# Entry of the short convolution: TensorE sums the meta rows, VectorE begins with tile 0

## The reference, cut to what matters

```python
h = jnp.concatenate([meta, x], axis=1)          # 16 + 512 rows
for i in range(DEPTH):
    mixed = rglru_mixer(...) if i % N_MIXERS == 0 else shortconv_mixer(...)
    h = layer_norm(ALPHA * h + mixed, ln_g[i, 0], ln_b[i, 0])
    ffn = hierarchical_moe(h, ...)              # top 2 of 32 experts per row
    h = layer_norm(ALPHA * h + ffn, ln_g[i, 1], ln_b[i, 1])
return h[:, N_META:]

def shortconv_mixer(h, w_in, conv_w, w_out):
    u = h @ w_in                                # bg | cg | v, 1024 columns each
    zc = causal_depthwise_conv(cg * v, conv_w)  # 3 taps
    return (bg * zc) @ w_out
```

## Time and profile before

| | us |
|---|---|
| median of 3 runs | 2333.53 (2333.42 to 2335.18) |
| the profiled execution | 2330.78 |
| its span, first to last instruction | 2329.1 |
| TensorE busy | 2127.1 (91%) |
| VectorE busy | 708.6 (30%) |
| ScalarE busy | 523.0 (22%) |
| GpSimd busy | 300.2 (13%) |
| mean granted clock of TensorE | 0.958 of 2.4 GHz |

### The profile page before, as it was taken

How to read it: one execution, slowest core, us unless ns; L and a number is a source line. 1 busy time by engine, 2 the same in 40 slices (tenths; PEclk the granted TensorE clock), 3 DMA queues, 4 the chain that set the end, 5 groups by cost and what they waited for, 6 DMA issues and landing times. The chain is left out here.

```text
span 2329.1 us, 28490 instructions
## 1 busy us (share of the span) xinstructions
PE 2127.1 (91%) x11572; PEld 1220.6 (52%) x11572; DVE 708.6 (30%) x1558; ACT 523.0 (22%) x1219; POOL 300.2 (13%) x306
## 2 busy tenths in 40 slices
PE   7999999999999999969999898959996999989991
PEld 3446643434545687445555454457754555545550
DVE  1055325343665455452111010151125211101104
ACT  2123221122553145112212112130001212121111
POOL 0000000221332311101111111031000111111101
PEclk9999998999999999979999999979997999999996
DMA  9315242222002222159999999962134999999993
GB/s 345 131 56 185 93 171 91 87 94 72 1 24 90 91 76 76 25 214 395 426 423 423 425 423 416 402 256 90 37 117 176 364 424 424 422 423 424 422 404 137
DMA packets 100664, 545.97 MB, mean 234 GB/s; under 512 B 13376, under 2 KB 27497, under 8 KB 66586
## 3 DMA queue, kind: packets, MB, share of 16 engines
q1 hardware_dynamic: 80950, 504.17, 53.7%
q0 software_dynamic: 19232, 39.56, 4.8%
q10 hardware_dynamic: 340, 0.28, 0.0%
HBM read 538.86 MB, written 28.94 MB: 244 GB/s over the span
## 5 line engine op out<-in xcount | busy, mean ns | idle before, releaser
L751 PE MATMUL ps<-arena,ring 128*128 128x512 f32 (+10 forms) x1968 | 589.9, 460 | 10.6 <-DVE arena L2181 2.2
L751 PEld LDWEIGHTS ps<-arena,ring 128*128 128x128 f32 (+2 forms) x1968 | 354.7, 191 | 233.9 <-issue 192.9
L1210 PE MATMUL ps<-ring,arena 128*64 128x256 f32 x3296 | 375.2, 384 | 6.1 <-ACT arena L1634 3.2
L1210 PEld LDWEIGHTS ps<-ring,arena 128*64 128x64 f32 x3296 | 233.9, 138 | 127.6 <-issue 4.6
L832 PE MATMUL ps<-ring,arena 128*128 128x512 f32 (+1 forms) x560 | 248.1, 600 | 4.9 <-ACT arena L1600 2.6
L1223 PE MATMUL ps<-ring,arena 128*64 128x512 f32 x880 | 206.0, 611 | 26.6 <-DMA ring<-in_moe_w_down_dram 26.6
L2287 DVE SCALAR_TENSOR_TENSOR arena<-arena,ps 128x256 f32<-128x256 f32 x78 | 32.8, 421 | 565.2 <-ACT arena L1644 565.2
L1210 PE MATMUL ps<-arena 128*64 128x256 f32 x1696 | 192.6, 381 | 0.0
L2564 POOL DMA_INDIRECT assignment_rows<-arena x78 | 81.6, 1046 | 797.1 <-ACT arena L1650 754.3
L832 PEld LDWEIGHTS ps<-ring,arena 128*128 128x128 f32 (+1 forms) x560 | 102.3, 186 | 137.7 <-issue 136.7
L1210 PEld LDWEIGHTS ps<-arena 128*64 128x64 f32 x1696 | 119.4, 137 | 60.5
(11 more groups left out here) (312 smaller groups left out, 1825.3 us busy)
## 6 DMA issues: line engine op xcount, KB each, us to landing
ring<-in_moe_w_down_dram SPq DMA_DIRECT2D x45, 2048.0 KB, 27.9
ring<-in_moe_w_up_dram SPq DMA_DIRECT2D x44, 2048.0 KB, 30.8
ring<-in_moe_w_gate_dram SPq DMA_DIRECT2D x43, 2048.0 KB, 25.9
arena<-in_moe_w_gate_dram SPq DMA_DIRECT2D x21, 2048.0 KB
arena<-in_moe_w_up_dram SPq DMA_DIRECT2D x20, 2048.0 KB
arena<-in_moe_w_down_dram SPq DMA_DIRECT2D x19, 2048.0 KB
ring<-in_ada_w_dram SPq DMA_DIRECT2D x12, 2048.0 KB, 8.7
ring<-in_a_w_in_dram SPq DMA_DIRECT2D x12, 1536.0 KB, 11.6
```

The costliest lines, as they stand in the source:

```text
L751: ins = pe.matmul(dst, w, m, start=i == 0, stop=i == len(pairs) - 1)
L1210: ins = pe.matmul(ps[CAP * i:CAP * (i + 1), bank_, 256 * j:256 * (j + 1)], rows_t[:, k, :], w[:, k, 256 * i:256 * (i + 1)], start=k == 0, ...
```

## The change

Tile 0 now comes first, then meta, 1, 2, 3 (`COMBINE_0`), on VectorE, ScalarE, GpSimd and for TensorE's turns; SP still loads meta's outputs first. For the meta tile VectorE's two passes are gone. Behind the routing VectorE makes two diagonal 16x16 matrices of the meta rows' gates (`meta_gates`), and TensorE, as soon as `yin[4]` has landed, sums in PSUM: identity times `X` of meta, plus each diagonal times the expert outputs, in two halves of 512 columns. VectorE takes the statistics from PSUM after tile 0's, and ScalarE normalises meta out of PSUM. ScalarE normalises every tile in two halves of 512 columns, each of which releases `normed` by 1. Its copies of tile 0 and meta stand together behind meta's normalisation, those of tile 1 behind the normalisation of tile 2, those of tiles 2 and 3 at the end. TensorE runs the early products of `cg_0` before tile 1's turn and those of `cv_0` after it; both now wait for meta's copies.

```diff
@@ -266,6 +266,7 @@
 UNITS_A = [(0, 2 * c + i, n) for c in range(GC) for n in range(NT) for i in range(2)] + \
     [(g, h, None) for g in (1, 2) for h in range(HPG)]
 NUA = len(UNITS_A)
+COMBINE_0 = (0, 4, 1, 2, 3)
 NUB = HB * NT
 
 
@@ -413,6 +414,7 @@
         slot_of = at(M0 + 20, 10).rearrange("p (t k) -> p t k", k=2)
         place = at(M0, 10 * 2)
         picked = at(M0 + 32, 2 * 5 * NE).rearrange("p (k t n) -> p k t n", k=2, n=NE)
+        meta_gates = at(R0 + 13520, 2 * META).rearrange("p (k i) -> p k i", k=2)
         emptied = at(M0 + 6400, NBLK)
         row_hot = at(M0 + 576, 10 * P).rearrange("p (i r) -> p i r", r=P)
         block_hot = at(M0 + 1856, 10 * NBLK).rearrange("p (i b) -> p i b", b=NBLK)
@@ -508,16 +510,16 @@
         def rows_of(tile):
             return META if tile == 4 else P
 
-        LN_TILES = [(l, t) for l, ts in ((0, range(4)), (1, range(4)), (2, (4, 0, 1, 2, 3)), (3, (4, 0, 1, 2, 3)),
+        LN_TILES = [(l, t) for l, ts in ((0, range(4)), (1, range(4)), (2, (4, 0, 1, 2, 3)), (3, COMBINE_0),
                                          (4, range(4)), (5, range(4))) for t in ts]
         LN = {k: i for i, k in enumerate(LN_TILES)}
         LN_DONE = {}
         for k in LN_TILES:
             if k[0] not in (2, 4):
                 LN_DONE[k] = len(LN_DONE) + 1
-        COMBINED = {k: i for i, k in enumerate(k for k in LN_TILES if k[0] in (3, 5))}
-
-        TURNED = {k: i for i, k in enumerate((k, t) for k in range(6) for t in (((4,) if 2 <= k <= 4 else ()) + (0, 1, 2, 3)))}
+        COMBINED = {k: i for i, k in enumerate(k for k in LN_TILES if k[0] in (3, 5) and k != (3, 4))}
+
+        TURNED = {k: i for i, k in enumerate((k, t) for k in range(6) for t in (COMBINE_0 if k == 4 else ((4,) if 2 <= k <= 3 else ()) + (0, 1, 2, 3)))}
 
         def taken(eng, name):
 
@@ -681,6 +683,8 @@
                         sp.wait_ge(*consumed(PREV[turn]))
                     if turn == first + RING:
                         sp.wait_ge(*((yT_ready, DC) if l == 0 else (comb_done, COMBINED[(3, 3)] + 1)))
+                        if l:
+                            sp.wait_ge(meta_sum, 1)
                     if turn == first + RING + 1:
                         done(sp, f"router{l}_3")
                     if turn == first + RING + 2:
@@ -806,14 +810,14 @@
                         ins = product(b[0:m, c0 - s0:c1 - s0], [(w[:, k, cols_], HT[:, k, c0:c1]) for k in range(DC)])
                 return ins
 
-            def start_early(jobs, k, t=2, lo=0, hi=SPLIT):
+            def start_early(jobs, k, t=2, lo=0, hi=SPLIT, ahead=0):
 
                 for h in range(2):
                     pe.wait_ge(turn_copied[h], TURNED[(k, t)] + 1)
                 for i, (name, turn, w, cols_, moving) in enumerate(jobs):
                     if lo == 0:
                         landed(pe, turn)
-                        started[name] = begin(name, i)
+                        started[name] = begin(name, ahead + i)
                     chunk(started[name], w, cols_, moving, P, lo, hi)
 
             def feature_major(name, w, cols_, moving, m=P):
@@ -1313,10 +1317,19 @@
             HALVES = ((META - 2, META - 2 + 257), (META - 2 + 257, TM))
             first = [(f"{n}_0", t, shaped(t, DC, 512), slice(0, P), HALVES)
                      for n, t in (("cg", TURN[("sc_in", 0, (1, 0))]), ("cv", TURN[("sc_in", 0, (2, 0))]))]
+            pe.wait_ge(meta_diag, 2)
+            pe.wait_ge(alpha_done, 5)
+            pe.wait_ge(yin_in[4], 16)
+            for h in range(2):
+                s = slice(512 * h, 512 * h + 512)
+                ins = product(ps[0:META, h, :], [(ident[0:META, 0:META], meta_x[0:META, s])] +
+                              [(meta_gates[0:META, k, :], yin[4][0:META, k, s]) for k in range(2)])
+            ins.then_inc(meta_sum, 1)
+            turn_tile(4, 0)
             turn_tile(4, 4)
-            turn_tile(4, 0)
+            start_early(first[:1], 4, 4, 0, META + P)
             turn_tile(4, 1)
-            start_early(first, 4, 0, 0, META + P)
+            start_early(first[1:], 4, 4, 0, META + P, ahead=1)
             turn_tile(4, 2)
             start_early(first, 4, 1, META + P, HALVES[1][0])
             turn_tile(4, 3)
@@ -1427,11 +1440,11 @@
 
             def combined_and_turned(k, l, order):
 
+                turns = {1: order[:2], 3: order[2:3], 4: order[3:]}
                 for i, t in enumerate(order):
                     deviation(l, t)
-                    if i:
-                        turn_copy(k, order[i - 1])
-                turn_copy(k, order[-1])
+                    for s in turns.get(i, ()):
+                        turn_copy(k, s)
 
             def sums(t):
 
@@ -1454,10 +1467,11 @@
                 r, o = rows_of(t), 32 * (n % 2)
                 act.activation(spec[0:r, o + 15:o + 16], spec[0:r, o + 14:o + 15], ACT.Sqrt).then_inc(sd_ready, 1)
                 if l == 3:
-                    m = COMBINED[(l, t)]
-                    act.wait_ge(scale_ready, m + 1)
-                    act.activation(X[0:r, t, :], X[0:r, t, :], ACT.Identity, scale=spec[0:r, o + 16:o + 17],
-                                   bias=spec[0:r, o + 17:o + 18]).then_inc(normed, 2)
+                    act.wait_ge(scale_ready, COMBINE_0.index(t) + 1)
+                    for h in range(2):
+                        s = slice(512 * h, 512 * h + 512)
+                        act.activation(X[0:r, t, s], ps[0:r, h, :] if t == 4 else X[0:r, t, s], ACT.Identity,
+                                       scale=spec[0:r, o + 16:o + 17], bias=spec[0:r, o + 17:o + 18]).then_inc(normed, 1)
 
             def first_turn_copy(t, h):
 
@@ -1692,7 +1706,7 @@
 
             route(0)
             experts(0)
-            combined_and_turned(4, 3, (4, 0, 1, 2, 3))
+            combined_and_turned(4, 3, COMBINE_0)
             for c in range(DC):
                 done(act, f"cg_{c}")
                 if c >= 2:
@@ -2380,10 +2394,20 @@
                     vec.scalar_tensor_tensor(x[:, s], x[:, s], inv, lnp[:, 1, s], ALU.mult, ALU.add).then_inc(ln_done, 1)
 
             route(0)
+            settle()
+            for k in range(2):
+                vec.tensor_scalar(meta_gates[:, k, :][0:META], ident[0:META, 0:META], gates[0:META, k, 4:5], None, ALU.mult)\
+                   .then_inc(meta_diag, 1)
             experts(0)
-            order = (4, 0, 1, 2, 3)
-            for i, t in enumerate(order):
-                combine(0, t, (lambda: scaled(order[i - 1])) if i else None)
+            combine(0, 0)
+            vec.wait_ge(meta_sum, 1)
+            for h in range(2):
+                o = 32 * (LN[(3, 4)] % 2)
+                mark(vec.bn_stats(spec[0:META, o + 6 * h:o + 6 * h + 6], ps[0:META, h, :]))
+            scaled(0)
+            variance(3, 4)
+            for t, last in ((1, 4), (2, 1), (3, 2)):
+                combine(0, t, lambda: scaled(last))
             scaled(3)
             turn_copy(4, 3)
 
@@ -2632,7 +2656,7 @@
             for t in (4, 0, 1, 2, 3):
                 rows_out(0, t)
             experts(0)
-            combined(0, (4, 0, 1, 2, 3))
+            combined(0, COMBINE_0)
             load_lnp(4)
             for t in range(NT):
                 rows_out(1, t)
```

More of the change, by code:

```diff
@@ L452, in build @@
         rot_in = sem("rot_in")
-        meta_back = sem("meta_back")
+        meta_back, meta_diag, meta_sum = (sem(n) for n in ("meta_back", "meta_diag", "meta_sum"))
         x_in, meta_in, x_back, x1_out, x1_back = (sem(n) for n in ("x_in", "meta_in", "x_back", "x1_out", "x1_back"))
```

## The result

| | before | after |
|---|---|---|
| median of 20 runs, us | 2332.53 (2326.82 to 2335.79) | 2337.09 (2332.37 to 2342.69) |
| ratio of the times | | 1.0022, 95% interval 1.0016 to 1.0029 |
| the profiled execution, us | 2330.78 | 2339.62 |
| its span, us | 2329.1 | 2337.9 |
| first load of experts' rows to third early block, us | 33.06 (1520.98 to 1554.04) | 38.48 (1523.72 to 1562.20) |

The ratio is +5.1 us (3.7 to 6.8): slower by just over 0.2%. The last line, called **the stretch** from here on, is the figure to work with. Single executions differ by several us ahead of the stretch (SP issues the first load 2.74 us later in the profile of after, where only the two small matrices are new in front; over all the profiles here it is issued between 1517.44 and 1525.32), and behind it the work is the same. The stretch grew by 5.42 us and the span by 8.8: 2.74 lies ahead, some 0.6 behind.

What follows compares the result with a forecast made beforehand. The start of the third early block on TensorE decides; ScalarE's chain, after a 0.5 us wait for the sum, moves it from 1554.0 to 1556.0, +2.0 us: median 2335.5, range 2332 to 2339 (8 in 10).

Steps and rivals of the forecast that it cites:

- rival A: TensorE's sum of meta rows stays at half clock, ends 1534.3, everything after 2.8 us later: +4.75, 2338.3; chance 0.23.
- Slower by over 0.2%: Whole kernel: measured slower by more than 0.2% (4.7 us), through a cold sum with dear halves or scatter; chance 0.12.
- The clock rises 5 us into the sum: TensorE's sum of meta rows: starts at half clock, full after 5.0 us, ends 1531.5; VectorE waits 0.5 us.
- The size of one cold record: TensorE's sum: one record of 512 columns takes 0.44 us at full clock, so 0.88 at half clock.
- The halves: ScalarE's normalisation: each pass of 512 columns takes 0.69 us, 0.24 us more a tile than one whole pass.
- ScalarE as the chain: ScalarE's passes and copies set the third early block: 1556.0 against 1554.04; TensorE waits 1.6 and 0.4 us.
- The first early products start 0.7 us earlier: TensorE's first early products start at 1541.9 instead of 1542.59, after ScalarE's copies of tile 0 and meta.
- Tile 0's first pass: VectorE takes up tile 0 at 1526.96, just after its rows land, instead of 1527.99.
- The diagonal matrices: VectorE's two 16x16 operations behind the routing cost nothing, as VectorE stands idle there for 4.85 us.
- Rival B: TensorE's own work binds, not ScalarE's: third early block at 1553.6, -0.5 us, 2333.0; chance 0.10.
- C: Whole kernel: half-microsecond effects cancel or scatter covers them, within 1 us of 2333.5; chance 0.15.
- a difference over 5 us: Whole kernel: sign that the prediction is wrong, a difference that it said no step here can make.

Runs made afterwards that it cites:

- 128 columns of weights: The changed kernel with stationary matrices of 16 rows by 128 columns in the sum, the added columns zero; ratio to before 1.0022 (1.0013 to 1.0030).
- nine products ahead: The changed kernel with nine products of 128x512 that nobody reads in front of the sum; ratio to before 1.0030 (1.0019 to 1.0041).
- three repairs: The changed kernel with four 128x512 products before the sum, whole ScalarE passes, five 128x128 products before the second early block; ratio to before 1.0005 (0.9996 to 1.0015).
- four products ahead: The changed kernel with four products of 128x512 that nobody reads in front of the sum; ratio to before 1.0011 (1.0003 to 1.0020).
- the order alone: The kernel before with only the tile order 0, meta, 1, 2, 3, VectorE still summing meta; ratio to before 1.0011 (1.0002 to 1.0020).

## Why the prediction was right and where it was wrong

The time, 2337.09, lies inside the range of 2332 to 2339, but the course of events was not the forecast's. It was rival A's, which had 0.23, and the range held because it was drawn to take in A. The forecast of 2335.5 was 1.6 us low, by the ratio (+5.1 against +2.0) 3.1; part of the nearness is luck, since the median of before came out 1.0 us under the one that the forecast was added to. Slower by over 0.2%, to which the text gave 0.12, is what the ratio says, though its interval reaches down to 0.16%.

- **"The clock rises 5 us into the sum": this step failed.** It rested on two rises under products with weights of 128 rows (by 128 columns in the earlier trace rows, by 64 in the earlier trace rows), and those of the sum have 16 rows and 16 columns. It ran at 0.50 for 10.4 us, ended at 1536.9 where its start at 1526.49 plus 7.75 (by the prediction's own rule) would be 1534.2, and VectorE waited 3.39 us in place of 0.5. Rival A had 10.6 us and 3.3. The Trainium skill (TensorE: Matmul & The Clock Gate, What's actually happening) says that activity releases the throttle; by that rule, as the prediction read it, A was out. The rows decide against that reading: the same engine, busy without a gap, kept the low clock in the change and with 128 columns of weights, and lost the high one with nine products ahead.
- **The size of one cold record was right**: 0.88 estimated from full-clock records, 0.85 measured; at full clock 0.44 and 0.43.
- **The halves were right**: 0.69 predicted, 0.71 measured. Alone they cost 0.44, in the change 0.8.
- **ScalarE as the chain was right up to the second block.** Tile 1's reciprocal waited 2.16 us (2 to 3 predicted), and the second early block stood behind ScalarE's copies for 2.04 us (1.6). The third did not: 0.4 us of waiting were predicted, and it followed tile 3's turn without any, since TensorE at half clock had become the slower one. The forecast was +2.0 with 0.5 us of waiting for the sum, so +1.5 without; with the sum at full clock it came to +2.50, of which 1.20 is the second fall, so +1.3.
- **The second fall was in no case.** The prediction let TensorE wait 1.6 us and counted it as free. It cost 1.2 us of clock behind it. It is the missing term of A, whose +4.75 is 1.5 for the chain and 3.3 for the cold sum: 1.3, 2.92 and 1.20 were measured, 5.42 together.
- **"The first early products start 0.7 us earlier" fell with the sum**: from SP's first load they came 1.44 us later (23.05 against 21.61). Tile 0's first pass started 5.45 us after that load; 5.98 was forecast from the earlier trace rows, and the other kernels with the new order have 5.33 to 6.31.
- **The diagonal matrices were free**, as the idle time of the earlier trace rows had it. VectorE made them in 0.38 us and still waited 4.57 us for TensorE:

```profile
1038.59 0.38 DVE L2399 TENSOR_SCALAR arena<-ident,arena 16x16 f32<-16x16 f32 x2
1043.55 1.36 DVE L2353 TENSOR_SCALAR arena<-ps,arena 128x128 f32<-128x128 f32 x4 [4.57 <-PE ps L1207]
```

- **Rival B** (TensorE keeps the lead) is out: TensorE waited 2.04 us for ScalarE after the first early product. **C** is out at +5.1. The "wrong" sign of a difference over 5 us, which "no step here can make", was reached by the ratio (+5.1) and by the stretch (+5.42), and the step that made it was the second fall.

## What to carry to other kernels

Don't count on products with few rows to raise TensorE's clock. Here products of 16 rows stayed at 0.50 for 10.4 us without a gap, and entered at 1.00 they lost it, in the middle of the run or at its end. Price them at the half clock when the engine comes from idle. When work moves from a busy engine to an idle one, compare the lengths on the path: here 2.6 us of VectorE (its two passes; the statistics stayed) became 10.4 us of TensorE. And an idle time on TensorE between products can have a second price, in the clock of what follows: here 1.2 us behind a wait of 2 us. Last, before adding up steps of a few tenths, look for what scatters inside the measured stretch: here the landing of one load, by up to 1.0 us.

## What the runs showed that was not expected

- Six f32 products of 16x16 by 512 columns: 10.39 us busy of 10.41, clock 0.50. With 128 columns of weights the same. Entered at 1.00, the clock fell 4.4 us later in the middle of them, in another kernel 5.1 us later inside the last record, and in the kernel with three repairs just behind the last, 5.4 us after the first. Weights of 128 rows by 64 columns did raise it, so the rows are the likely property, but a sum with 128 rows was not tried.
- The clock's rise under the early products came 3.0 us after their start at the earliest (four products ahead) and 6.1 at the latest (128 columns of weights). In the change this hides under ScalarE's chain; in before and in the order alone it moves the third block.
- The second fall: 0.50 for 3.4 us behind a wait of 2.04 us between products with weights of 128x128, and none in the profiles with 0.60 to 1.28 us. What decides it, and whether it comes in every execution of the change, is open, since there is one profile of each kernel.
- TensorE starts nothing for over 5 us behind the last expert product of layer 0, even with work that waits for nothing visible (5.27 to 5.64 us in the four kernels that have products there), and ScalarE's first instruction there, a table load, stands behind 5.45 us in the change; the profile names no releaser. It lies under the wait for the experts' rows in both kernels. Its cause was not looked into.
